# Block one's experts with token tiles of 32 in four column groups, and several steps around them moved

## The reference, cut to what matters

```python
MEM_TOKENS = 256
N_GROUPS = 4
EXPERTS_PER_GROUP = 8
TOP_K_IN_GROUP = 2
D_EXPERT = 256
...
    for g in range(N_GROUPS):
        a = jnp.einsum('td,edf->tef', t, w_gate[g])
        b = jnp.einsum('td,edf->tef', t, w_up[g])
        m = jax.nn.silu(a) * b * combine[:, g, :, None]
        y = y + jnp.einsum('tef,efd->td', m, w_down[g])
...
def _mem_xattn(hx, hm, w_mq, w_mkv, w_mo):
    q = (hx @ w_mq).reshape(B, S, MEM_HEADS, MEM_HEAD_DIM)
    k, v = jnp.split(hm @ w_mkv, 2, axis=-1)
    ...
    x = x + _mem_xattn(_rms(x, cross_norm_g[l]), _rms(mem, mem_norm_g[l]), w_mq[l], w_mkv[l], w_mo[l])
```

## Time and profile before

| what | value |
|---|---|
| median of 3 runs | 1034.42 us (1033.56 to 1035.21) |
| the profiled execution: its time | 1035.14 us |
| its span | 1033.1 us |
| PE busy | 986.1 us, 95% of the span |
| DVE busy | 583.6 us, 56% |
| ACT busy | 352.2 us, 34% |
| read from HBM | 287.34 MB, 279 GB/s over the span |
| mean granted clock of PE | 0.988 of full |

### The profile page before, as it was taken

The page is one execution under the profiler, slowest core; times in us unless marked ns, Lnnn a source line. Parts: engine busy times, 40 slices in busy tenths (PEclk is TensorE's granted clock), DMA queues, the critical chain, the costliest instruction groups (busy, mean ns, idle before and its releaser), DMA issues.

```text
span 1033.1 us, 14969 instructions
## 1 busy us (share of the span) xinstructions
PE 986.1 (95%) x5320; PEld 593.7 (57%) x5320; DVE 583.6 (56%) x1110; ACT 352.2 (34%) x679; POOL 21.1 (2%) x41
## 2 busy tenths in 40 slices
PE   8999999999999899999999999999899999999985
PEld 7678566977967533443443479876763434434434
DVE  5834437555345546445445475678675655555556
ACT  5654324455445222222222354754441111111113
POOL 1000001000000000000000000000000000000000
PEclk9999999999999899999999999989999999999998
DMA  9263492446407499999999927350619999999931
GB/s 360 120 250 137 195 397 102 163 183 243 166 1 319 180 362 427 424 425 424 428 423 429 397 83 324 141 228 1 245 62 385 423 427 424 426 424 426 424 153 41
DMA packets 28895, 289.04 MB, mean 280 GB/s; under 512 B 3080, under 2 KB 5544, under 8 KB 7728
## 3 DMA queue, kind: packets, MB, share of 16 engines
q1 hardware_dynamic: 25344, 282.04, 66.4%
q0 software_dynamic: 1136, 3.74, 1.1%
q10 hardware_dynamic: 2368, 2.64, 0.8%
HBM read 287.34 MB, written 1.06 MB: 279 GB/s over the span
## 4 chain that ended last, share of the span: by engine, by line
PE 82%; DVE 9%; ACT 3%; DMA 3%; issue 2%; DVEq 0%; SPq 0%; POOL 0%; ACTq 0%; POOLq 0%
PE bank L997 23%; PE bank L1011 11%; PE bank L627 7%; PE bank L628 6%; PE bank L629 6%; PE bank L1017 6%; PE bank L1004 4%; DVE ring_r L484 2%; PE bank L720 2%; PE bank L752 2%; PE bank L972 1%; PE bank L733 1%; PE bank L604 1%; DMA ring<-in_lat 1%; DMA HT<-in_rel_bias 1%
## 5 line engine op out<-in xcount | busy, mean ns | idle before, releaser
L997 PE MATMUL bank<-ring,arena 128*64 128x512 f32 x1040 | 237.5, 598 | 0.2 <-DVE arena L2218 0.2
L2248 DVE TENSOR_REDUCE arena<-bank 128x512 f32 x130 | 83.7, 686 | 117.3 <-PE bank L1017 114.8
L484 DVE TENSOR_TENSOR ring_r<-ring,ring_r 128x1024 fp32r<-128x1024 f32 (+1 forms) x84 | 99.2, 1211 | 85.1 <-ACT ring_r L477 85.1
L997 PEld LDWEIGHTS bank<-ring,arena 128*64 128x64 f32 x1040 | 69.1, 136 | 122.7 <-issue 122.7
L1011 PE MATMUL bank<-ring,arena 128*64 128x512 f32 x520 | 125.8, 604 | 0.5 <-DVE arena L2263 0.3
L477 ACT ACTIVATE ring_r<-ring 128x1024 fp32r<-128x1024 f32 (+1 forms) x84 | 84.8, 1046 | 78.8 <-PE bank L629 77.2
L627 PE MATMUL bank<-HT_r,ring_r 128*128 128x256 f32 x352 | 101.2, 288 | 5.4 <-issue 2.1
L629 PE MATMUL bank<-HT_r,ring_r 128*128 128x256 f32 x352 | 99.6, 283 | 0.0
L1590 ACT ACTIVATE arena<-bank 128x512 f32<-128x512 f32 x64 | 38.3, 598 | 147.6 <-PE bank L997 147.6
L1017 PEld LDWEIGHTS bank<-tab,arena 128*128 128x128 f32 x520 | 55.7, 140 | 54.8 <-issue 49.6
L1017 PE MATMUL bank<-tab,arena 128*128 128x128 f32 x520 | 70.9, 279 | 3.3 <-DVE arena L2277 2.1
(11 more groups left out here) (436 smaller groups left out, 1431.5 us busy)
## 6 DMA issues: line engine op xcount, KB each, us to landing
ring<-in_experts SPq DMA_DIRECT2D x64, 2048.0 KB, 14.8
ring<-in_experts SPq DMA_DIRECT2D x64, 1024.0 KB, 11.1
ring<-in_ada SPq DMA_DIRECT2D x12, 2048.0 KB, 10.1
ring<-in_win SPq DMA_DIRECT2D x5, 2048.0 KB, 11.4
ring<-in_hy SPq DMA_DIRECT2D x3, 2048.0 KB, 19.5
ring<-in_mk SPq DMA_DIRECT2D x2, 2048.0 KB, 11.1
ring<-in_mv SPq DMA_DIRECT2D x2, 2048.0 KB, 10.5
ring<-in_wo SPq DMA_DIRECT2D x2, 2048.0 KB, 7.3
```

The lines of the kernel that those rows point to most:

```text
L484: nc.vector.tensor_tensor(R(w), w, R(h), ALU.subtract).then_inc(sem("w_low"), 1)
L997: last = mm(gu_bank[g:g + WIN, :], xw[:, k, :], w[:, k * 512:(k + 1) * 512], start=k < 2, stop=k >= KD - 2)
L2248: last = V.reduce_sum(ysT[:, 4 * u:4 * u + 4, bass.ds(s, WIN)], dT_bank[u][:, :].rearrange("p (c g w) -> p c w g", c=4, g=2), AXX)
```

## The change

Block one's experts (b = 1) take windows of 32 pairs, and product k goes to column group k mod 4. The four down products go to the four column groups of one bank, which four transposes turn. The list of extra passes has 16 places for block one. Each step of block one gets four matmuls nobody reads. `bias` moves behind `swT`; `mem` gets a buffer of its own, is loaded at head 0, squared at heads 3 and 4 and scaled at head 5, and `memT` stands ahead of `convolve(1)`; `ada(3)` moves behind `convolve(0)`. `gx` begins with three banks token tile by token tile; `g2r` moves ahead of block two's counts; the scatter waits for one half at a time; the first `token_sums` moves from head 0 to head 1; numbers of fillers and bank places change. Block two's experts keep windows of 64.

```diff
-WIN = 64
+WIN = {1: 32, 2: 64}
+NX = {b: NPAIR // w for b, w in WIN.items()}
...
-STAGES += [("cv1", 2), ("memT", 4), ("mk", 4),
+STAGES += [("memT", 4), ("cv1", 2), ("mk", 4),
+EXPERT = {1: (5, 6, 7, 0), 2: (4, 5, 6, 7)}
+SUMS = {1: (1, 2, 3, 4), 2: (0, 1, 2, 3)}
...
@@ PE, heads of block one
-                if h < 6:
+                if h < 6 and h != 2:
                     ada(h + 1)
+                if h == 3:
+                    ada_col(3)
...
+                if h >= 6:
+                    occupy(f"pv{h}", 0, 1)
...
                     convolve(0)
+                    ada(3)
...
+            transposed("memT", mem, KD, "xn_m")
             convolve(1)
-            transposed("memT", XN, KD, "xn_m")
-            occupy("mk", 0, 5)
@@ PE, moe
-                    occupy("rT2", 0, 17)
+                    occupy("rT2", 0, 18)
...
-                occupy(f"cnt{b}", 0, 10 if b == 2 else 8)
+                occupy(f"cnt{b}", 0, 6 if b == 2 else 8)
+                if b == 2:
+                    gate_row("g2r", diag2, "diag2")
...
-                if b == 1:
-                    pe.wait_ge(sem("onehot"), 32)
-                    ps = take(pe, "bias")
...
-                occupy(f"gx{b}", 0, 4 if b == 2 else 6)
-                pe.wait_ge(sem(f"sel{b}"), TT)
+                occupy(f"gx{b}", 0, 6)
+                gx = [take(pe, f"gx{b}", k) for k in range(3)]
+                for t in range(TT):
+                    pe.wait_ge(sem(f"sel{b}"), t + 1)
+                    for k in range(3):
+                        gather(k, t)
...
+                if b == 1:
+                    pe.wait_ge(sem("onehot"), 32)
+                    ps = take(pe, "bias")
...
-                occupy(f"yTa{b}", 0, 2)
+                occupy(f"yTa{b}", 0, 2 if b == 2 else 1)
@@ PE, one expert
-                        g = 64 * (k % 2)
-                        last = mm(gu_bank[g:g + WIN, :], xw[:, k, :], w[:, k * 512:(k + 1) * 512],
-                                  start=k < 2, stop=k >= KD - 2)
+                        g = wide * (k % sides)
+                        last = mm(gu_bank[g:g + wide, :], xw[:, k, :], w[:, k * 512:(k + 1) * 512],
+                                  start=k < sides, stop=k >= KD - sides)
...
-                            last = mm(d_bank[half][64 * f:64 * f + WIN, :], hb[:, f, :], w[:, o:o + 512],
+                            g = wide * (f if b == 2 else 2 * half + f)
+                            last = mm(d_bank[half if b == 2 else 0][g:g + wide, :], hb[:, f, :], w[:, o:o + 512],
...
                         gu_T().then_inc(sem(f"guT_done{b}"), 1)
+                        if b == 1:
+                            for _ in range(4):
+                                mm(d_bank[1][:, 0:256], ident, T("iota")[:, 0:256], start=True, stop=True)
@@ PE, scatter
-                    for half in range(2):
-                        ready(pe, stage, 2 * (pt % 2) + half)
-                    for t in range(TT):
-                        for half in range(2):
+                    for q in range(4):
+                        t, half = (q // 2, q % 2) if end else (q % 2, q // 2)
+                        ready(pe, stage, 2 * (pt % 2) + half)
@@ PE, beside
                 if h == 0:
-                    pe.wait_ge(sem("squared"), 4)
-                    token_sums(lss, sq, range(4), (0,))
+                    occupy("ap0", 0, 2)
                 elif h == 1:
                     wp_lru(0, 0)
+                    full(token_sums(take(pe, "lss"), sq, range(4)), "lss")
@@ ACT, heads of block one
-                if h + 2 == H1 - 1:
-                    act.dma_start(XN, A["mem"].rearrange("(t p) d -> p t d", p=P)).then_inc(sem("mem_in"), 16)
+                if h == 0:
+                    act.wait_ge(sem("product"), TT)
+                    act.dma_start(mem, A["mem"].rearrange("(t p) d -> p t d", p=P)).then_inc(sem("mem_in"), 16)
+                if h in (3, 4):
+                    square(junk_m, three(mem[:, h - 3, :], 2), ssq_m[:, h - 3:h - 2])
@@ DVE
                 if h == 5:
+                    normalised("m", lambda t: mem[:, t, :], lambda t: mem[:, t, :], rstd_m, "xn_m")
                     spectrum_product(1)
-            normalised("m", lambda t: XN[:, t, :], lambda t: XN[:, t, :], rstd_m, "xn_m")
             low(dve, "mk0", (0, 1))
+            low_evac("memT", HT, low_x, 4, lambda k: C("mem_norm_g", k))
             gated(1)
...
-                    for k in range(2, S // WIN):
+                    for k in range(2, S // wide):
```

More of the change, by code:

```diff
@@ L49 @@
 NPAIR = 2 * S
[L50 to L52 removed]
+WIN = {1: 32, 2: 64}
+PAD = 64
+SORTED = NPAIR + PAD
+NX = {b: NPAIR // w for b, w in WIN.items()}
+XSTART, XEXPERT, XCOUNT = NE, NE + 16, NE + 32
 RING = 4
@@ L521, in two_blocks @@
         pair_w = route(NPAIR // P)
-        mk8, tm8, mk8b = [three(route(NX * NE), NX) for _ in range(3)]
-        xst, xid = route(NX), route(NX)
+        mk8, tm8, mk8b = [{b: three(XNf[:, 512 * q:512 * q + n * NE], n) for b, n in NX.items()} for q in range(3)]
+        xst, xid = [XNf[:, q:q + 16] for q in (1536, 1552)]
         block = ctx.enter_context(nc.Block())
@@ L764, in ada_col @@
                                   start=True, stop=True)
+                    if a + 1 < len(parts):
+                        mm(ps[:, 256:512], ident, T("iota")[:, 0:256], start=True, stop=True)
                 full(last, f"adac{i}")
@@ L982, in moe @@
                     full(last, f"swT{b}", j)
-                occupy(f"yTa{b}", 0, 2)
+                if b == 1:
+                    pe.wait_ge(sem("onehot"), 32)
+                    pe.wait_ge(sem("mask_row"), 1)
+                    ps = take(pe, "bias")
+                    full(mm(ps[0:H1, :], relb[0:BUCKETS + 1, :], oneh[0:BUCKETS + 1, :], start=True, stop=True), "bias")
+                occupy(f"yTa{b}", 0, 2 if b == 2 else 1)
                 for k in range(KD):
@@ L1221, in beside @@
                 if h == 0:
[L1222 to L1225 removed]
+                    occupy("ap0", 0, 2)
                 elif h == 1:
[L1227 removed]
                     pe.wait_ge(sem("lo_low"), 1)
                     wp_lru(0, 0)
+                    pe.wait_ge(sem("squared"), 4)
+                    full(token_sums(take(pe, "lss"), sq, range(4)), "lss")
                 elif h == 2:
@@ L1434, in _ @@
             for h in range(H1):
-                if h < 6:
+                if h == 3:
+                    ada_evac(3)
+                if h < 6 and h != 2:
                     ada_evac(h + 1)
@@ L1548, in moe @@
                 A_(R(xn_high[:, 1, :]), XN[:, 1, :], ACT.Copy).then_inc(sem("xn_high"), 1)
+                if b == 2:
+                    for k in range(KD):
+                        last = A_(diag2[:, k, :], ident, ACT.Copy, scale=mod[:, 40 + k:41 + k])
+                    last.then_inc(sem("diag2"), 1)
                 act.wait_ge(sem("e_diff"), b)
@@ L1553, in moe @@
                 if b == 2:
-                    for k in range(KD):
-                        last = A_(diag2[:, k, :], ident, ACT.Copy, scale=mod[:, 40 + k:41 + k])
-                    last.then_inc(sem("diag2"), 1)
                     copies("g2r", [g2row[:, 0:512], g2row[:, 512:1024]])
-                if b == 1:
-                    ps = got(act, "bias")
-                    free(A_(brow[0:H1, :], ps[0:H1, :], ACT.Copy), "bias")
-                    ready(act, "bias")
-                    act.dma_start(bias_rows, brow[0:H1, :]).then_inc(sem("bias_out"), 16)
                 for k in range(0, KD, 2):
@@ L1575, in moe @@
                     last.then_inc(sem("x_high"), 1)
+                if b == 1:
+                    ps = got(act, "bias")
+                    free(A_(brow[0:H1, :], ps[0:H1, :], ACT.Copy), "bias")
+                    ready(act, "bias")
+                    act.dma_start(bias_rows, brow[0:H1, :]).then_inc(sem("bias_out"), 16)
                 for j in range(2):
```

193 lines of the change are left out of this document (106 added, 87 removed).

## The result

| | before | after |
|---|---|---|
| median of the runs, us | 1034.58 (1033.56 to 1035.21, 4 runs) | 1005.79 (1005.37 to 1007.53, 4 runs) |
| span of the profiled execution, us | 1033.1 | 1003.7 |
| mean granted clock | 0.988 | 0.996 |
| PE busy, us | 225.0 of the experts' 226.2 | 183.4 of the experts' 217.65 |

The ratio is 0.9726, with a 95% interval from 0.9709 to 0.9743. Beside the last experiments the changed kernel was timed once more: 1007.58 us (1005.79 to 1009.08, 5 runs) against 1034.49, ratio 0.9730 (0.9714 to 0.9746). The forecast was 1005.2 us, in a range from 999 to 1017. The sum came out right. Its largest term did not, and two gains stood in the code without a term.

The account below looks back on a forecast made before the run. PE was taken to bound block one's experts, transfers close behind. Terms of -12.6, -6.0, -3.0, -3.2, -2.4 and -2.0 sum to -29.2, from 1035.1 to 1005.9, 1005.2 us for the median; range 999 to 1017.

Parts of the forecast that it names:

- The bound: Block one's experts: PE bounded before with the transfers close behind; after the change the transfers bound, PE waiting 1.6 us a step.
- The experts' term: Block one's experts: the stage, then bound by transfers at 425 GB/s, takes 213.6 us against 226.2, -12.6 us.
- The last down product takes 0.9.: End of block one's experts: 0.9 us added behind the transfers, within the stage's sum of 213.6 us.
- Counts to the first expert: Block one, ahead of the experts: `bias` no longer delays the gather and DVE's evictions set the start, -6.0 us.
- Head 2: `ada(3)` moved behind the convolution finds its weights landed; its wait and the low clock behind it go, -3.0 us.
- the memory: From `memT` to `mk`: transposes ahead of `convolve(1)`, which covers their evictions, -3.2 us.
- The first `token_sums`: Near 690 us: a filler replaces the products of one column, which move behind denser work, ending a half clock, -2.0 us.
- Behind the experts and at the end: Fewer last transposes in block one, scatter waiting for one half, block two's last turning begun on its first half: -2.4 us.
- turn the stage round: Rival, block one's experts: PE's waits bring half clock throughout, step 11.5 us, 1162 us in all; chance 0.03 for slower.
- A low clock now and then: Rival: the experts' last step and part of the scatter run at half clock, +4 us, 1009, inside the forecast's own range.
- fall to 410: Rival: transfers run at 410 GB/s, adding 7.4 us, 1013 us; chance 0.20 for 1011 to 1018, shared with another case.
- No extra pass: Rival: an expert with over 32 pairs costs another pass, three outweighing the stage's gain; expected none in block one, chance 0.01.

Follow-up runs that it names:

- The experiment: The changed kernel with the product for `bias` back between the counts and the gather, its old bank and ACT's copy too: 1010.42 us, ratio 0.975.
- its experiment: The changed kernel with two stages' banks exchanged, so that `ak`'s first half stands in bank 7 again: 1009.54 us, ratio 0.9752.
- four other edits: The changed kernel with the first `token_sums`, `bias`, `ada(3)`, `memT` and `ak`'s bank as before: 1023.08 us, ratio 0.9888.

## Why the prediction was right, and where not

**The bound.** Right: PE bounded with the transfers close behind, and now the transfers do, at 426 GB/s where 425 was taken. The step is 7.38 us, forecast 7.40. Gate and up take 1.92, PE's own step 5.75, forecast 5.77.

**The experts' term** is the step that failed, in one addend: "The last down product takes 0.9." The issue of the second pair was forecast 8.0 us behind the first product and came at 8.02; the last landing works out at 556.38 + 1.049 MB / 426 GB/s = 558.8, forecast 345.2 + 8.0 + 202.3 + 2.4 = 557.9. Then the down product was taken to start at once. But expert 31's gate-and-up part lands 2.5 us ahead of its down part, and it takes 5.4 us more to the down product. So the stage ends 4.0 us behind the last landing, not 0.9. 0.9 and 3.1 us are the 4.0 by which -12.6 became -8.6. (The landing's 0.9 is about what the queue's gap costs: from 354 to 356 us it moves 254 GB/s instead of 426, 0.8 us worth.) In a stage that PE bounds, nearly all of the 5.4 us is PE's own work and is counted in its steps; with the transfers as the bound it stands behind a landing and has to be added. Loading the gate-and-up parts first gives it 4.9 us of cover and nearly closes the gap in the queue. It took 3.25 us back, by the bytes about 2.5 of it from the order of the last loads and the rest from the gap; the two weren't tried apart. -8.6 lies between the ends that the term was given, -14 and -5.2, but those were made for the first bytes and the rate, and not for this.

**Counts to the first expert**: -5.7, forecast -6.0. The size is right and the reason half. The forecast moved `bias` and derived the rest from DVE's chain as it stands in block two. The experiment gives 2.8 for `bias`. A further 1.9 lies between `swT` and the first expert, most of it a wait for `swT`'s bank (1.57 us) that the new list of banks takes away, and the forecast had not read it. The remaining 0.9 is read from the marks too and wasn't tried by itself: even with `bias` ahead the gather starts 9.7 and not 10.2 us behind the counts, its fillers taking 4.32 instead of 5.49, and it takes 0.4 less.

**Head 2** -3.0, **the memory** -3.6, both as forecast. With `ada(3)` back, though, the cost is 5.3, probably since the memory's early load delays its weights; then each edit's price depends on the other.

**Banks.** The edit of the list of banks got no term. It was worth 2.1 us at `yl`, as its experiment shows, and most of 1.9 ahead of the experts, as the traces suggest. A bank is a resource with a queue of its own: whoever takes it next waits for the last reader. The diff shows the list, and the trace of before shows the two gaps of PE.

**The first `token_sums`** -3.1, forecast -2.0, at the far end of its own bounds (-3.2): nearly all of the half clock came back, and nothing behind it absorbed it. It was undone only together with four other edits, where its stretch took 3.1 us more. Three of the experiments' executions, though, had 5 us at 0.66 to 0.73 near there, worth 1.5 us, with `token_sums` where the change puts it. So half of the gain is not certain in each run.

**Behind the experts and at the end**: -1.8 and -2.0, forecast -2.4 for both together. In block two the marks put -0.4 ahead of the extra pass's down product, the last one, and -1.5 behind it, at the transposes and the scatter. Which of the edits there brings it wasn't tried apart.

**The rivals.** The clock did not turn the stage round: 21 waits of 1.5 to 1.7 us, 32.8 us in all, and not one slow product. With waits of 3.4 us it turned every second step, and even so the time rose by some 2 us: the slow products fell into time that PE would have waited. A step with its fillers at half the clock, the rival's 11.5 us, was never seen; nothing here forces it. "A low clock now and then" is seen, at the first expert in three traces. The transfers did not fall to 410: they ran at 426 from 400 to 560 us, and at 417 over the whole stage with its start. No extra pass ran in block one: the page counts 1040 instructions on L1025, 16 for an expert, so 65 experts' worth, block two's one extra pass among them.

So the total was right by luck: errors cancelled. The forecast had 4.0 us too much in the experts and 0.3 at the counts, and too little in the banks (2.1), in `token_sums` (1.1) and behind the two expert parts (0.5 and 0.9). That leaves 0.3 of 29.4. (The memory's 0.4 too little is made up by 0.4 between `mk` and the counts.) The repeated timing of the same kernel, 1007.58 us, lies 2.4 above the forecast, so an agreement to 0.6 says little by itself.

## What to carry to other kernels

When an edit hands the bound from an engine to the transfers, add to the sum everything that stands between the last landings and the stage's end, the engine's own last products included, because it no longer lies beside other steps; then order the loads so that what starts it lands first. Compare a step with the transfers over the whole stage, the loads that the ring holds at its start counted: here the two are level at 6.8 us, not at the 7.4 that one expert's bytes take. And read a list of banks as you read a queue.

## What the hardware showed beyond expectation

Without fillers the clock and the waits locked into a pattern of two steps: a wait of 3.37 us, products at half the clock (3.51 and 3.64 us), a wait of 1.6 us, products at full clock. The mean clock was 0.84 to 0.86 for 200 us, and the step stayed at 7.4.

The clock at the first expert differs between executions of one program. In the changed kernel it was full in the first profile (1.92 us for the first gate and up) and half in the second (3.27 us). Of the twelve profiled kernels with tiles of 32, nine took 1.92 us, and three took 3.3 to 3.5. These three had a product on 33 rows (`bias`) and one filler just ahead of it, but so had most of the nine; why the clock fell in some stays open.
